# Gating sums in a recurrent/attention stack: sums over tiles added on GpSimd, one product with ones per sum, and the gating steps three beats nearer to the last tile of v

## The reference, cut to what matters

```
h = rms_norm(x, norm1_g[l])
q, k, v, gu, gv = split(h @ w_in[l])               # q 1024, k 256, v 256, gu 1024, gv 1024
attn = banded_window_attention(q, k, v, sink)       # after norm and rotation of q, k
sgu = chunked_spatial_gating(gelu(gu), gelu(gv), ln_g, ln_b, w_s, b_s)
mixed = concat([rms_norm(attn, attn_out_g), rms_norm(sgu, sgu_out_g)])
x = x + mixed @ w_o[l]
x = x + conv_gated_ffn(rms_norm(x, norm2_g[l]), ...)

def chunked_spatial_gating(u, v, ln_g, ln_b, w_s, b_s):
    vn = layer_norm(v, ln_g, ln_b)                  # mean and variance over 1024 channels
    f = einsum('hpq,bcqhd->bcphd', w_s, vn) + b_s   # positions mixed in chunks of 128, 8 heads
    return u * f
```

## Time and profile before

| | |
|---|---|
| median of three runs | 3545.67 us |
| profiled execution, its own time | 3542.9 us |
| its span, first to last instruction | 3541.1 us |
| PE busy | 3474.8 us, 98% |
| DVE busy | 2738.2 us, 77% |
| ACT busy | 1887.5 us, 53% |
| POOL busy | 1701.3 us, 48% |
| mean granted PE clock | 0.996 |

### The profile page before, as it was taken

The page is one execution under the profiler, slowest core; times in us unless marked ns, Lnnn a source line. Parts: engine busy times, 40 slices in busy tenths (PEclk is TensorE's granted clock), DMA queues, the critical chain, the costliest instruction groups (busy, mean ns, idle before and its releaser), DMA issues.

```text
span 3541.1 us, 53042 instructions
## 1 busy us (share of the span) xinstructions
PE 3474.8 (98%) x19584; PEld 2992.7 (85%) x19584; DVE 2738.2 (77%) x4083; ACT 1887.5 (53%) x2857; POOL 1701.3 (48%) x1473
## 2 busy tenths in 40 slices
PE   8999999999999999999999999999999999999999
PEld 7887788888877788887888888888888888888888
DVE  8768887679989976687888758877688888658875
ACT  6555785455555554675544434444665544444443
POOL 4324672267778742144466406653143666306640
PEclk9999999999999999999999999999999999999999
DMA  5544456555555556644555665556544555665566
GB/s 191 168 155 143 160 181 186 187 187 171 180 165 169 174 161 189 194 143 129 187 186 189 183 189 188 186 183 190 188 138 143 189 185 187 186 187 189 186 184 179
DMA packets 177042, 624.39 MB, mean 176 GB/s; under 512 B 19784, under 2 KB 25616, under 8 KB 175760
## 3 DMA queue, kind: packets, MB, share of 16 engines
q1 hardware_dynamic: 171216, 606.11, 54.5%
q10 hardware_dynamic: 5568, 14.89, 1.1%
HBM read 618.75 MB, written 2.17 MB: 175 GB/s over the span
## 4 chain that ended last, share of the span: by engine, by line
PE 72%; DVE 10%; POOL 5%; issue 2%; ACT 2%; ACTq 0%; POOLq 0%; DVEq 0%
PE psG L533 43%; PE psG L531 23%; DVE WL L1275 3%; PE psG L530 3%; POOL SQ L1742 1%; ACT WH L770 1%; POOL SQ L1761 1%; DVE sdx L1288 1%; POOL sdx L1744 1%; POOL GV L1883 1%; DVE Et L1545 1%; DVE Et L1552 1%; PE psM L556 0%; DVE Y L1280 0%; PE psM L514 0%
## 5 line engine op out<-in xcount | busy, mean ns | idle before, releaser
L533 PE MATMUL psG<-H,WH 128*128 128x512 f32 x5655 | 2022.4, 398 | 0.0
L1275 DVE TENSOR_TENSOR WL<-RAW,WH 128x1024 fp32r<-128x1024 f32 (+1 forms) x1162 | 1495.9, 1287 | 518.1 <-ACT WH L770 516.7
L770 ACT ACTIVATE WH<-RAW 128x1024 fp32r<-128x1024 f32 (+1 forms) x1162 | 1214.1, 1045 | 869.2 <-PE psG L533 849.2
L531 PE MATMUL psG<-H,WL 128*128 128x256 f32 x6032 | 1663.5, 286 | 0.2
L533 PEld LDWEIGHTS psG<-H,WH 128*128 128x128 f32 x5655 | 1066.9, 189 | 234.0
L531 PEld LDWEIGHTS psG<-H,WL 128*128 128x128 f32 x6032 | 1143.9, 190 | 44.5 <-issue 9.6
L533 PE MATMUL psG<-Y,WH 128*128 128x512 f32 x2792 | 988.8, 397 | 0.0
L531 PE MATMUL psG<-Y,WL 128*128 128x256 f32 x2944 | 802.1, 281 | 1.0 <-DVE Y L1280 1.0
L533 PEld LDWEIGHTS psG<-Y,WH 128*128 128x128 f32 x2792 | 524.6, 188 | 119.2
L531 PEld LDWEIGHTS psG<-Y,WL 128*128 128x128 f32 x2944 | 555.6, 189 | 15.9 <-issue 1.4
L1892 POOL TENSOR_SCALAR fou<-fsu,PAR 128x256 f32<-128x256 f32 x88 | 177.9, 2022 | 564.6 <-DVE fsu L1317 564.6
(11 more groups left out here) (352 smaller groups left out, 3616.0 us busy)
## 6 DMA issues: line engine op xcount, KB each, us to landing
RAW<-in_w_up SPq DMA_DIRECT2D x352, 512.0 KB, 3.6
RAW<-in_w_o_in SPq DMA_DIRECT2D x162, 512.0 KB, 3.7
RAW<-in_w_e_in SPq DMA_DIRECT2D x128, 512.0 KB, 3.6
RAW<-in_w_down SPq DMA_DIRECT2D x128, 512.0 KB, 3.5
RAW<-in_w_in SPq DMA_DIRECT2D x112, 512.0 KB, 3.6
RAW<-in_w_o SPq DMA_DIRECT2D x72, 512.0 KB, 3.6
RAW<-in_w_e_out SPq DMA_DIRECT2D x64, 512.0 KB, 4.6
RAW<-in_w_o_out SPq DMA_DIRECT2D x64, 512.0 KB, 4.3
```

The source lines that it names most:

```text
L531: ins = e.matmul(o[:, 0:T], wl, x[:, 0:T], start=False, stop=False, skip_group_check=True)
L533: ins = e.matmul(o, wh, x, start=False, stop=last)
L770: copy = lambda o, i, scale=1.0: e.activation(o, i, ACT.Copy, scale=scale)
L1275: tt(WL_[c % NRAW][:, 0:n], RAW_[c % NRAW][:, 0:n], WH_[c % NW][:, 0:n].bitcast(F32), SUB).then_inc(sem("wl"), 1)
```

## The change

The mean's sum and the last sum of squares are formed differently. For the mean, POOL copies the first gelu tile of gv to `gacc` (the tile `v2[0]`, which V has left by then, so its name is v in rows) and adds the other seven one by one, four beats behind the end of each tile; PE then makes one product with ones at s0+4. For the last sum, POOL copies the first square and adds seven, one a beat, and PE makes one product three beats behind the last `sgm`. The sum of the squares of the centred gv stays with PE, 8 products.

The event `sgu` moves from 7 to 4 beats behind the last tile of gv (s0 from 971 to 968 in the first layer), and with it all that counts from s0. The transposes are spaced by `i * 3 // 2` beats for `i * 5 // 4`. `SPLIT` goes from 12 to 13. The steps behind the last sum are two beats further from the last `sgm`, which itself comes three beats earlier. Waits on the constants' two loads are joined in one semaphore, and two semaphores of the second norm as well.

```
-SPLIT = 12
+SPLIT = 13
-        s0 = S.end_of("gv", l * 8 + 7) + 7
+        s0 = S.end_of("gv", l * 8 + 7) + 4
-            S.event("sgt", l * 8 + i, s0 + 21 + i * 5 // 4)
+            S.event("sgt", l * 8 + i, s0 + 21 + i * 3 // 2)
+    gacc = v2[0]
...
 PE, gating(b):
+            for l in at("sgu", b - 4):
+                w.wait_ge(sem("gv_sum"), 8 * l + 8)
+                colsum(("mu", l), gacc)
             for k in range(4):
-                for l in at("sgu", b - 1 - k):
-                    w.wait_ge(sem("gelu"), l * 16 + 8)
-                    for i in (2 * k, 2 * k + 1):
-                        sums(("mu", l), i, GV[i], 8)
...
-            for u in at("sgm", b - 1):
-                w.wait_ge(sem("gu_sq"), u + 1)
-                sums(("suq", u // 8), u % 8, gq[u % 4], 8)
+            for u in at("sgm", b - 3):
+                if u % 8 == 7:
+                    w.wait_ge(sem("gu_sum"), u + 1)
+                    colsum(("suq", u // 8), gacc)
...
 ACT, gating(b): root of suq at sgm b - 4 (was b - 2), copies to Y at b - 7 - i // 2 (was b - 5 - i // 2)
 DVE, gating(b): scaling at sgm b - 6 - i // 2 (was b - 4 - i // 2), low half at b - 8 - i // 2 (was b - 6 - i // 2)
...
 POOL, attention(b):
+            for i in at("gv", b - 4):
+                l, k = divmod(i, 8)
+                w.wait_ge(sem("gelu"), 16 * l + k + 1)
+                if k == 0:
+                    w.wait_ge(sem("small"), small[("suq", l - 1)].done) if l else None
+                    e.tensor_copy(gacc, GV[0]).then_inc(sem("gv_sum"), 1)
+                else:
+                    w.wait_ge(sem("gv_sum"), 8 * l + k)
+                    tt(gacc, gacc, GV[k], ADD).then_inc(sem("gv_sum"), 1)
+            for u in at("sgm", b - 1):
+                l, i = divmod(u, 8)
+                w.wait_ge(sem("gu_sq"), u + 1)
+                if i == 0:
+                    w.wait_ge(sem("small"), small[("mu", l)].done)
+                    e.tensor_copy(gacc, gq[0]).then_inc(sem("gu_sum"), 1)
+                else:
+                    w.wait_ge(sem("gu_sum"), u)
+                    tt(gacc, gacc, gq[i % 4], ADD).then_inc(sem("gu_sum"), 1)
```

More of the change, by code:

```diff
@@ L572, in lstm @@
                 gates_add(16 + y, v_s[y % 3])
-                w.wait_ge(sem("idn"), 16)
+                w.wait_ge(sem("con"), 32)
                 use = take(("vt", y))
@@ L866, in halves_of @@
                     w.wait_ge(sem("small"), small[("vv", i - 2)].done)
+                    w.wait_ge(sem("small"), small[("suq", i // 2 - 1)].done)
                 half("V", i)
@@ L1064, in norms @@
                     w.wait_ge(own.sem, own.n)
-                    e.activation(ft, rl, ACT.Exp, scale=-0.5).then_inc(sem("fin_r2"), 1)
+                    e.activation(ft, rl, ACT.Exp, scale=-0.5).then_inc(sem("fin_rms"), 1)
         def ssd(b):
@@ L1210, in gating @@
                             w.wait_ge(sem("small"), sum_done[(("gvq", l), i - 4)])
+                        elif l:
+                            w.wait_ge(sem("gu_sum"), 8 * l)
                         e.activation(gq[i % 4], GV[i], ACT.Square).then_inc(sem("gv_sq"), 1)
@@ L1221, in gating @@
                 w.wait_ge(sem("gu_m"), u + 1)
-                w.wait_ge(sem("small"), small[("gvq", l)].done if i < 4 else sum_done[(("suq", l), i - 4)])
-                e.activation(gq[u % 4], GU[i], ACT.Square).then_inc(sem("gu_sq"), 1)
-            for u in at("sgm", b - 2):
+                w.wait_ge(*((sem("small"), small[("gvq", l)].done) if i < 4 else (sem("gu_sum"), u - 3)))
+                e.activation(gq[i % 4], GU[i], ACT.Square).then_inc(sem("gu_sq"), 1)
+            for u in at("sgm", b - 4):
                 if u % 8 == 7:
@@ L1228, in gating @@
             for i in range(8):
-                for u in at("sgm", b - 5 - i // 2):
+                for u in at("sgm", b - 7 - i // 2):
                     if u % 8 == 7:
@@ L1410, in heads @@
                 w.wait_ge(sem("h_exp"), h + 1)
-                w.wait_ge(sem("cmk"), 16)
+                w.wait_ge(sem("con"), 32)
                 for a, E in ((0, E0), (1, E1)):
@@ L1489, in norms @@
                 if r == 31:
-                    w.wait_ge(sem("fin_r2"), 1)
+                    w.wait_ge(sem("fin_rms"), 2)
                     tt(rstd, fr, ft, MUL).then_inc(sem("rstd"), 1)
@@ L1664, in gating @@
             for i in range(8):
-                for u in at("sgm", b - 4 - i // 2):
+                for u in at("sgm", b - 6 - i // 2):
                     if u % 8 == 7:
@@ L1670, in gating @@
                         stt(GU[i], GU[i], par(f"pc{l}", "sog", i), gr, MUL, MUL).then_inc(sem("gu_n"), 1)
-                for u in at("sgm", b - 6 - i // 2):
+                for u in at("sgm", b - 8 - i // 2):
                     if u % 8 == 7:
@@ L1932, in sync @@
         fetch(3)
-        e.dma_start(ident, I["c_ident"]).then_inc(sem("idn"), 16)
-        e.dma_start(cmask, I["c_cmask"]).then_inc(sem("cmk"), 16)
+        e.dma_start(ident, I["c_ident"]).then_inc(sem("con"), 16)
+        e.dma_start(cmask, I["c_cmask"]).then_inc(sem("con"), 16)
         e.dma_start(PAR[1][:, 0:columns("pb")[1]], I["pb"]).then_inc(sem("pb"), 16)
```

## The result

| | before | changed |
|---|---|---|
| median of the runs | 3544.22 us (8 runs, 3539.77 to 3546.02) | 3533.62 us (8 runs, 3532.91 to 3536.44) |
| profiled execution, its own time | 3542.9 us | 3532.99 us |
| its span | 3541.1 us | 3531.2 us |

The ratio is 0.9974, with a 95% interval of 0.9964 to 0.9985, which is 9.2 us faster (5.3 to 12.8 us); the two medians lie 10.6 us apart. The profiled executions differ by 9.9 us. The forecast was 3530.2 us, with 15.5 us between two profiled executions; the kernel is faster, the time lies in the range, and 5.6 us of the forecast gain are missing between the profiled executions. The question is where they went. The median missed by less, 3.4 us, and that part is luck: the forecast added 2.8 us to get from a profiled execution to the median, which was 0.6 us in the changed kernel.

A forecast was written before the change was run, and what follows sets the result against it. PE, busy nearly all the time, was taken as the bound. Terms -12.0 - 1.6 - 1.5 - 0.4 = -15.5 us took the profiled 3542.9 to 3527.4; 2.8 more gave a median of 3530.2 us, range 3522 to 3538.5.

The forecast's parts named there:

- The products removed: PE's products with ones in both layers: 28 go, each worth 0.43 us, -12.0 us.
- late squares: Last sum on PE: its waits for ACT's squares of GU go, -1.6 us in all.
- What POOL gets: 4 copies and 28 additions on POOL, in time for PE and hidden on DVE: cost 0.
- First, the squares: PE's wait for gating's first squares falls from 1.1 us a layer to 0.3: -1.5 us in two layers.
- Second and third, the chain and the clock: Gating up to PE's second product with `w_s`: waits -2.2 us, low clock behind it in both layers +1.8, together -0.4.
- `SPLIT` 13 and the later steps: Behind the last sum: two beats later paid by the earlier event, tiles read at beat 1022, DVE's extra additions fit idleness.
- The products saved ahead of the chain: Rival, chance 0.16: the mean's saved products are given back in the chain's wait; only -7.6 us, 3538.1 us.
- DVE did not become the bound: Rival denied here, chance 0.03: 32 POOL operations hold DVE, its low weights reach PE late; +9.5 us, 3555.2 us.
- the rule that the prediction weighed: SBUF: two-input VectorE and GpSimd instructions exclude each other; at worst each POOL addition holds DVE for its full length.

The follow-up runs named there:

- The doubled kernels: Changed kernel with an unused second POOL addition ahead of each of the 32 new operations: 3542.13 us; ahead of the mean's only: 3535.06; the last sum's only: 3538.33.

## Why the prediction was right, and where it was not

**The products removed: right within what can be told.** The 28 products are gone. With the beats of before the sums alone took 11.5 us off the stretch, where 13.6 were forecast for products and late squares and 0.9 came back as a wait for the last sum. Of the 1.2 us that are left, the longer wait for the attention's tiles takes 0.6 (0.7 to 1.3). The other 0.6 have no place that I can show; the products at 0.43 each are the right size.

**What POOL gets: nearly right, by less than the text has it.** The mean's sum was in time. That DVE's loss beside it would stay hidden was not quite so: 0.6 us of it reached PE at the attention's tiles. The last sum was 0.4 us late in one layer, though the text has it in time even at 1.6 us for each addition: they took 0.74 to 1.48 us, and each starts only when ACT's square comes. The doubled kernels show how near it stands: one more operation a beat costs 4.7 us there.

**First, the squares: this step failed.** The text has: "I expect 0.3 at the last pair". It was 2.6 in each layer, and that is the step that put the forecast off. The six squares do stand ahead of the root, as said, but the tanh of gu's third tile stands ahead of the fifth, and that tile came late, because its scaling on DVE and its polynomial on POOL stand behind the centring on both. So the root began late and the last pair stood behind all of it. In place of -1.5 us that is +3.0, and the first layer has a stretch at the lower clock behind it that no term counts, 1.4 us (from the start of the four products to the fourth block behind them 3.49 us, against 2.13 in the second layer). Moving only the root away took the wait out and 4.7 us off the stretch, so the root's part is shown; the late tanh's part is read from the timelines. The lower clock did not follow this wait in every kernel.

**Second and third, the chain and the clock: right.** Forecast was a wait of 4.4 us in each layer at the second product with `w_s`; measured are 3.8, with 0.5 at a transposition. A stretch at the lower clock follows in both layers. Chain and clock together were to give -0.4 us; the waits for POOL and ACT show -0.9, and 0.5 us of waiting for DVE at the products with `w_s`, which the kernel before had, is gone too. The clock fell once in each layer before as well, so here it adds nothing.

**The account.** Products -12.0, GU's squares -1.6, first squares +3.0, the chain's waits -1.4, POOL's sum +0.4, the attention's tiles +0.6, one more stretch at the lower clock +1.4: -9.6 us, where the stretch shows -10.3 and the profiled executions -9.9. Against the forecast the squares miss by 4.5 and their clock by 1.4 us, together 5.9, where 5.6 are missing; the waits for the sum and for the attention's tiles (1.0 worse) and the chain (1.0 better) cancel.

**`SPLIT` 13 and the later steps, priced at nothing: right for this change, and only in its company.** The old beats with SPLIT 12 cost 7.5 us of the stretch (1345.2 against 1337.7): 4.0 us of waits at `Y` and two more stretches at the lower clock.

**The rivals.** The products saved ahead of the chain were not absorbed: with the beats of before their gain arrives nearly in full. DVE did not become the bound, but it does pay: its lows beside the first layer's gv tiles grew from 1252 ns on average before (51.3 us for 41) to 1283 with POOL's sum and 1359 with the sum doubled. The eight doubled operations of that layer, 4.9 us at 612 ns each, made them 3 us longer in sum (41 times 76 ns), some 60% of POOL's time; DVE's other instructions are not in this count. Over both layers, 16 such operations cost the kernel 1.4 us by the medians and 3.3 in the stretch, of which 1.0 is the wait for `ax` and part of the rest the longer lower clock. By the rule that the prediction weighed (the Trainium skill, SBUF — State Buffer, section "Who interferes with whom"), where the loser is blocked for the whole instruction, it would be up to all 4.9 in a layer; the direction agrees, and the size is below that worst case here.

## What to carry to other kernels

A product with ones on the busy matrix engine is worth nearly its full length among the weights, and sums over tiles can go to GpSimd as long as one of its operations a beat is all that it gets; even then 0.4 to 0.9 us of waiting for the last sum and 0.6 at tiles of the vector engine came with it. Count in a moved chain not only the step itself but everything that stands ahead of it in the same engine's list, down to the tile whose data comes from a third engine; here a late tanh and a root ahead of two squares turned a gain of 1.5 us into a loss of 3. And try the parts apart before keeping them together: the moves by themselves gained nothing, the sums with SPLIT 13 at the old beats gained at least as much as the whole change, and shifting one root by two beats was worth more than the moves were.

## What was not expected of the hardware

- POOL's scalar step on one 128x256 tile took 0.41 us alone and 1.26 beside DVE's weights (line 1863), its copy 0.40 at gv's first tile and 0.88 at the first square, its additions of two tiles 0.73 to 1.48.
- Doubling sixteen operations on an engine that was 49% busy undid half of a change's gain; a mean share of busy time says nothing on whether there is room in a beat.
- In fourteen profiles the part of the program that no edit touches took from 2191.1 to 2196.3 us. It is as large as most effects here, and the length between two fixed instructions of PE tells more than the whole time.
- What stays open: whether the part outside the two layers varies by chance or with the kernel's code, 0.6 us of the products' term, why the clock fell behind the 2.6 us wait in some kernels and layers and not in others, and a list order for ACT that frees the transpositions of their 2.1 us in each layer without giving them to the products with `w_s`.
